# Dilated attention of a hybrid decoder step: turned rows first in each step, key rows copied by VectorE, first loads inside the projection, sample queries prepared in the last steps

## What is computed

```python
A_GROUPS = ((128, 1), (512, 4), (2048, 16))      # window, dilation; 8 heads of 64 each
def a_mixer(hn, pos, caches, w_in, q_g, k_g, w_out):
    n, T, _ = hn.shape
    qkv = (hn @ w_in).reshape(n, T, 3, N_GROUPS, A_HEADS, HEAD_DIM)
    for g, (window, dil) in enumerate(A_GROUPS):
        q = rope(rms_norm(qkv[:, :, 0, g], q_g[g]), pos)
        k = rope(rms_norm(qkv[:, :, 1, g], k_g[g]), pos)
        v = qkv[:, :, 2, g]
        if caches is None:
            o, lse = dilated_attention_prompt(q, k, v, window, dil)
            new = jnp.stack([k[:, T - keep:], v[:, T - keep:]], axis=1)
        else:
            o, lse, new = dilated_attention_sample(q, k, v, caches[g], window, dil)
...
    wts = jax.nn.softmax(jnp.stack(lses, axis=0), axis=0)
    o = jnp.einsum('gnthd,gnth->nthd', jnp.stack(outs, axis=0), wts.astype(outs[0].dtype))
    return o.reshape(n, T, A_HEADS * HEAD_DIM) @ w_out, rows
```

## Time and profile before

| what | us |
|---|---|
| median of 3 runs (lowest, highest) | 2953.03 (2950.44, 2971.38) |
| the profiled execution, its own time | 2953.42 |
| its span, first to last instruction | 2951.6 |
| busy in the span: TensorE, VectorE, ScalarE, GpSimd | 2710.9, 1736.7, 985.1, 725.0 |
| the stretch from the end of the projection to the first sample multiplication | 289.9 (520.4 to 810.26) |

### The profile page before, as it was taken

The page is one execution under the profiler, slowest core; times in us unless marked ns, Lnnn a source line. Parts: engine busy times, 40 slices in busy tenths (PEclk is TensorE's granted clock), DMA queues, the critical chain, the costliest instruction groups (busy, mean ns, idle before and its releaser), DMA issues.

```text
span 2951.6 us, 45737 instructions
## 1 busy us (share of the span) xinstructions
PE 2710.9 (92%) x17524; PEld 2636.7 (89%) x17524; DVE 1736.7 (59%) x2732; ACT 985.1 (33%) x1826; POOL 725.0 (25%) x342
## 2 busy tenths in 40 slices
PE   4999999788687999999999969698979999999997
PEld 3999999677676999999999958588979999999997
DVE  6887831555455555555555586695255655555655
ACT  3666631765303212221222245484222121112120
POOL 2111121333303222222222132173232222222220
PEclk7999999898788999999999989898999999999998
DMA  3322233443244343433354211344623444434441
GB/s 104 88 75 86 72 108 101 140 140 110 83 129 113 84 96 82 89 82 89 82 105 94 49 39 46 122 162 126 127 51 83 98 95 91 97 84 82 96 75 61
DMA packets 219856, 275.64 MB, mean 93 GB/s; under 512 B 29562, under 2 KB 191746, under 8 KB 217666
## 3 DMA queue, kind: packets, MB, share of 16 engines
q1 hardware_dynamic: 219746, 274.17, 37.2%
HBM read 237.90 MB, written 125.62 MB: 123 GB/s over the span
## 4 chain that ended last, share of the span: by engine, by line
PE 81%; DVE 8%; ACT 3%; DMA 3%; issue 2%; POOL 1%; SPq 1%; DVEq 0%; ACTq 0%; POOLq 0%
PE acc L347 23%; PE acc L349 23%; PE acc L348 23%; DVE arena L579 2%; PE aux L1869 2%; PE aux L1502 2%; PE acc L1461 1%; PE acc L1856 1%; PE acc L1470 1%; DVE arena L555 1%; PE acc L1839 1%; PE aux L635 1%; PE aux L634 1%; PE acc L2100 1%; POOL xl L533 1%
## 5 line engine op out<-in xcount | busy, mean ns | idle before, releaser
L347 PE MATMUL acc<-xh,w_hi 128*128 128x344 f32 x3504 | 1136.8, 324 | 63.4 <-DVE xl L533 36.3
L349 PE MATMUL acc<-xh,w_lo 128*128 128x344 f32 x3504 | 1127.8, 322 | 0.0
L348 PE MATMUL acc<-xl,w_hi 128*128 128x344 f32 x3504 | 1127.4, 322 | 0.0
L332 POOL TENSOR_TENSOR w_lo<-w_raw,w_hi 128x1024 fp32r<-128x1024 f32 x194 | 485.5, 2507 | 1799.9 <-ACT w_hi L322 1799.9
L347 PEld LDWEIGHTS acc<-xh,w_hi 128*128 128x128 f32 x3504 | 665.8, 190 | 82.0 <-issue 39.6
L349 PEld LDWEIGHTS acc<-xh,w_lo 128*128 128x128 f32 x3504 | 665.8, 190 | 0.0
L348 PEld LDWEIGHTS acc<-xl,w_hi 128*128 128x128 f32 x3504 | 665.8, 190 | 0.0
L849 DVE TENSOR_TENSOR hT<-hT,acc 128x1032 f32<-128x1032 f32 x184 | 226.3, 1230 | 387.6 <-PE acc L349 387.6
L322 ACT CAST w_hi<-w_raw 128x1024 fp32r<-128x1024 f32 x194 | 201.8, 1050 | 603.2 <-PE acc L349 504.3
L347 PE MATMUL acc<-f_hi,w_hi 128*128 128x344 f32 x1056 | 340.2, 322 | 11.1 <-DVE f_lo L1108 11.1
L349 PE MATMUL acc<-f_hi,w_lo 128*128 128x344 f32 x1056 | 339.5, 321 | 0.0
(11 more groups left out here) (254 smaller groups left out, 3184.6 us busy)
## 6 DMA issues: line engine op xcount, KB each, us to landing
out_a_w_sample<-in_cache_a_kv_w SPq DMA_DIRECT2D x23, 2848.0 KB
w_raw<-in_ffn_w_up SPq DMA_DIRECT2D x88, 512.0 KB, 3.8
scratch<-arena SPq DMA_DIRECT2D x46, 516.0 KB, 3.1
w_raw<-in_ffn_w_down SPq DMA_DIRECT2D x44, 512.0 KB, 3.5
w_raw<-in_a_w_in SPq DMA_DIRECT2D x36, 512.0 KB, 4.3
out_a_w_sample<-in_cache_a_kv_w SPq DMA_DIRECT2D x8, 2044.0 KB
arena<-in_cache_a_kv_w SPq DMA_DIRECT2D x24, 512.0 KB, 3.8
w_raw<-scratch SPq DMA_DIRECT2D x18, 512.0 KB, 3.7
```

Source lines behind the costliest of these rows:

```text
L332: pool.tensor_tensor(w_lo[:, slot, :], w_raw[:, slot, :], w_hi[:, slot, :].bitcast(F32), ALU.subtract).then_inc(lo_ready, 1)
L347: pe.matmul(out, whi, ahi, start=first, stop=False)
L348: pe.matmul(out, whi, alo, start=False, stop=False)
L349: return pe.matmul(out, wlo, ahi, start=False, stop=last)
```

## The change

It has four parts.

1. *Turned rows at the head of each step.* TensorE now turns value rows, key rows and statistics and spreads weights before the scores of unit k + 1, not behind them. VectorE makes half of unit k's masks, then the copies of value and key rows and the weighing, then the other half. The copy of key rows moves from ScalarE to VectorE (`key_rows_dve`). ScalarE's splits of keys and queries move from the head of the step to behind the second half of the exponentials.
2. *First loads in the projection.* Keys, queries and values of x = 0 are loaded at chunk 26 into the space of `rope` and `rinv`; ScalarE splits them at chunk 29 (`FIRST_SPLIT`), GpSimd two chunks later. x = 1 takes the place of x = 0 in the loads at chunk 35.
3. *The first scores' waits.* Units 0 and 1 wait only for those chunk thirds whose banks they take; VectorE clears the value tile between its half masks without waiting for the stores.
4. *Sample queries in the last steps.* `s_cols` is loaded at step 30 into `u_tail`; the queries are turned as jobs "sq" in steps 38 to 40 and split by VectorE; after step 42 (`A_TAIL` = 43) VectorE writes `s_sel` and TensorE makes the first two spreads; three of the first four cache loads are issued in steps 39 to 41, before the last statistics; the loads of the output weights no longer wait for the mixing.

```diff
         def proj_a_sp(sp):
-            with sp.Fori(0, A_CHUNKS // BODY - 1) as i:
+            with sp.Fori(0, 24 // BODY) as i:
...
-            for n in range(A_CHUNKS - BODY, A_CHUNKS):
+            for n in range(24, A_CHUNKS):
+                if n == 26:
+                    first_loads_sp(sp)
+                    first_values_sp(sp)
...
-                    sp.wait_ge(stored[0], 16 * 7)
-                    attn_a_loads(sp, 0, "q")
-                    attn_a_loads(sp, 0, "k")
+                    attn_a_loads(sp, 1, "q")
+                    attn_a_loads(sp, 1, "k")
...
+            if 38 <= k < 38 + NG:
+                names += [("sq", k - 38)]
...
-        ON_ACT = {"v": False, "k": True, "stat": True, "w": False}
+        ON_ACT = {"v": False, "k": False, "stat": True, "w": False, "sq": False}
...
         def raw_a(x, what):
-            return k_raw[x % 2] if what == "k" else q_raw
+
+            if x == 0:
+                return a_og["kqv".index(what)]
...
+        def first_loads_sp(sp):
+
+            sp.wait_ge(chunk_out, 3 * (CH + 24))
+            sp.wait_ge(stored[0], 16 * 12)
+            sp.wait_ge(stored[1], 16 * 12)
+            sp.dma_start(raw_a(0, "k"), rows_in_scratch(1, 0)).then_inc(DA.k_in[2], 16)
+            sp.dma_start(raw_a(0, "q"), rows_in_scratch(0, 0)).then_inc(DA.q_in[0], 16)
...
+                if k == 30:
+                    sp.dma_start(s_cols, scratch[0:A_CHUNKS, :, SEQ:T].rearrange("c p t -> p c t")).then_inc(ZA.cols, 16)
...
+                if k in (39, 40, 41):
+                    wait_job(sp, ("t", k - 2, 1))
+                    cache_rows_sp(sp, k - 39)
...
-                pe.wait_ge(acc_evac, 3 * CH_B)
+                pe.wait_ge(acc_evac, 3 * CH_B - (2 if u else 3))
...
-        def attn_a_pe(pe):
-            for k in range(-1, A_STEPS):
-                if 0 <= k + 1 < A_UNITS:
-                    scores_a_pe(pe, k + 1)
+        def attn_a_pe(pe, k0, k1):
+            for k in range(k0, k1):
...
+                if 38 <= k < 38 + NG:
+                    sample_rows_pe(pe, k - 38)
+                if 0 <= k + 1 < A_UNITS:
+                    scores_a_pe(pe, k + 1)
...
+        def key_rows_dve(v_, n):
+            cnt = K_JOBS[n % 4][3]
+            wait_job(v_, ("k", n))
+            if n < 2:
+                v_.wait_ge(lo_ready, U_AOUT + 2)
+            else:
+                v_.wait_ge(DA.k_out[n % 2], 16 * (n // 2))
+            v_.tensor_copy(k_stage[n % 2][:, 0:P * cnt], bank_a(("k", n))[:, 0:P * cnt]).then_inc(DA.out_dve, 1)
...
                 if k < A_UNITS:
-                    mask_a_dve(v_, k)
+                    mask_a_dve(v_, k, 0)
...
+                i, r = divmod(k, 10)
+                if 0 <= i < A_PAIRS and r in (2, 3, 6, 7):
+                    key_rows_dve(v_, 4 * i + (2, 3, 6, 7).index(r))
...
+                if 38 <= k < 38 + NG:
+                    sample_rows_dve(v_, k - 38)
+                if k < A_UNITS:
+                    mask_a_dve(v_, k, 1)
...
-                for x in starting(k + 3):
-                    if x:
-                        split_a_act(act, x, "k")
-                for x in starting(k + 2):
-                    if x:
-                        split_a_act(act, x, "q")
                 if 0 <= k < A_UNITS:
                     exps_a_act(act, k, 0)
-                i, r = divmod(k, 10)
-                if 0 <= i < A_PAIRS and r in (2, 3, 6, 7):
-                    key_rows_act(act, 4 * i + (2, 3, 6, 7).index(r))
...
+                for x in starting(k + 3):
+                    if x:
+                        split_a_act(act, x, "k")
+                for x in starting(k + 2):
+                    if x:
+                        split_a_act(act, x, "q")
```

More of the change, by code:

```diff
@@ L1578, in probs_a @@
             wait_job(eng, ("t", u, e))
+            if u == 0:
+                for n in range(2):
+                    eng.wait_ge(stored[n], 16 * A_CHUNKS // 2)
             if u >= 2:
@@ L2062, in sample_a_pe @@
                               start=True, stop=True)
-            pe.wait_ge(ZA.split, NG)
             for n in range(STEPS_A):
-                g, s2 = divmod(n, NS // 2)
                 if n >= 2:
-                    pe.wait_ge(ZA.multiplied, n - 1)
-                for e in range(2):
-                    for x in (s_qh, s_ql):
-                        mm = pe.matmul(acc[:, (2 * n + e) % 4, :], s_sel[:, 2 * s2 + e, :],
-                                       x[:, CROW * g:CROW * g + CROW], start=x is s_qh, stop=x is s_ql)
-                mm.then_inc(ZA.spread, 1)
+                    spread_pe(pe, n)
                 if 0 <= n - FIRST < PIECES // 2:
```

211 lines of the change are left out of this document (121 added, 90 removed).

## The result

The changed kernel takes **2982.24 us** (median of 8 runs, 2980.71 to 2984.28); the kernel before, on the same chip, 2954.51 us (median of 8). The ratio is 1.0075, 95% interval 1.0045 to 1.0105: 0.75% slower. Forecast were 2939.4 us and a range of 2919 to 2956; both are missed. The run with the profile took 2984.28 us, its span is 2982.5 us.

The account below looks back on a forecast made before the run. TensorE, with 81% of the chain and kept waiting in the attention, was taken to bound the kernel. Terms +1.7 + 1.2 - 2.5 - 2.0 + 0.7 - 1 - 11.7 = -13.6 us gave 2939.4 us from 2953.0; range 2919 to 2956.

Parts of the forecast that it names:

- start, to unit 10: From projection to unit 10's scores: earlier first scores, then waits for late query splits; +1.7 us (-6 to +5).
- block two: Attention units 10 to 19: old waits go, late splits add waits; 64.1 against 62.9 us, +1.2 us.
- block three: Attention units 20 to 29: old waits go, late splits add waits; 64.1 against 66.6 us, -2.5 us.
- units 30 to 38: Attention units 30 to 37, same trade of waits: 49.9 against 51.9 us, -2.0 us.
- last steps, statistics: Last attention steps: two cache loads now stand ahead of the last statistics' DMAs; +0.7 us (0 to +2).
- weights to first multiplication: Last weights, mixing and sample preparation: -1 us from a warmer clock, -11.7 us from sample work moved into the attention.
- the term for the clock: In each block of ten units: three waits lower TensorE's clock, 2.5 us added to 61.6 us.
- The wait that I let pay: At each group's scores: late splits cost 2 to 6 us, paid for by 9 us of old waits a block.
- The rival of late splits: Attention groups: late splits cost 2.5 us more each, 2967 us; sign turns at 1.2 us more a group; chance 0.12.
- The rival in which nothing takes the place of the waits: Attention blocks: splits run in ScalarE's idle time, so 26.2 us of waits simply go; 2912 us, chance 0.13.
- The sample term: Between mixing's end and first sample multiplication: preparation already done in the attention, only a product and hand-over left; -11.7 us.
- The third rival: Twelve sample steps: late cache rows or output weights stretch them, 8 us given back, 2947 us; chance 0.15.

Follow-up runs that it names:

- e5: Kernel after with two VectorE writes of 1024 columns ahead of the copy that leads to the last stage's first product: 2956.28 us.
- e6: Kernel before with three VectorE writes of 1024 columns ahead of the copy that leads to the last stage's first product: 2989.44 us.
- e1: Kernel after with ScalarE's splits of the next group's keys and queries ahead of the step's first exponentials again: 2919.81 us, ratio to before 0.9883.
- e12: e1 plus two dense pieces behind the last stage's first sparse products, and ScalarE's next output-weight split held until after the sample's small product: 2915.08 us.

## Why the prediction was wrong

By its own steps, forecast against measured in the profiled executions:

| step | forecast | measured |
|---|---|---|
| start, to unit 10 | +1.7 | +3.0 |
| block two | +1.2 | +5.9 |
| block three | -2.5 | +1.6 |
| units 30 to 38 | -2.0 | +1.1 |
| last steps, statistics | +0.7 | +3.6 |
| weights to first multiplication | -12.7 | -9.8 |
| the twelve sample steps, to the last stage | 0 | -2.1 |
| the last stage | not priced | +27.3 |

**The step that failed most** is one that the prediction doesn't have: it ends its sum at the sample steps and takes all behind them to keep its length, so the last stage is a term put at nothing without a reason. That stage starts 3.25 us later and took 82.3 instead of 55.0 us, since the clock stayed at its lower level; that a shift of its start alone does this is shown by e5 and e6. The earlier trace rows end at 849.50, ahead of it, and the prediction cites no row of the stage. In the profiled executions the kernel after lies 44.2 us behind the forecast at line 549 (30.6 + 13.6), and 27.3 of them are this; in the medians it is 42.8 us (2982.2 - 2939.4).

**The blocks.** The mechanism was right: waits for low halves at eleven groups, 25 to 50 us in all forecast, 40.9 measured; 3.9, 6 and 2 us for the three groups of a block forecast, 4.24, 5.27 and 1.02 measured. Mis-sized was above all the term for the clock, in a block that was forecast at 64.1 us and took 68.8. TensorE's busy time multiplied by the mean granted clock is nearly the same in all versions with rows first, 54.51 x 0.84 = 45.8 us in the kernel after, 50.77 x 0.91 = 46.2 in e1; so a block of the kernel after would take about 45.8 + 14.3 idle = 60.1 us at the full clock (61.6 forecast), and the clock costs about 8.7 us, where I had added 2.5. That is an estimate, since the mean also counts idle time. Not all of it belongs to the late splits: reckoned in the same way e1 loses 4.6 us a block (50.77 - 46.2) beside 5.5 us idle. I had taken the 2.5 us from the one block of before whose clock was 0.92; the one beside it was 0.85.

**The wait that I let pay.** The forecast set the late splits against the waits that go and came to -3.3 us for three stretches. The runs price them apart: 42.6 us for the late splits, against 31.1 us that all the rest gains. The 2 to 6 us a group were the forecast's own prices, and they were right for the waits (40.9 us over eleven groups is 3.7). The rival of late splits, which I gave 0.12, named the right place but asked for 2.5 us more a group. Up to unit 38 the kernel after is 13.1 us behind the forecast (+11.5 against -1.6), or 1.2 us a group: half of that rival, and just where its sign turns. The rival in which nothing takes the place of the waits (2912 us) is e1 and e12: 2919.8 and 2915.1 us, and it needed only the splits where they were.

**Smaller steps.** First scores at 519.63, within 1 us of the last projection product, right. The chain of the start was read well too: unit 4 at 537.7 and unit 8 at 558.2 forecast, 535.9 and 558.4 measured. The wait of the statistics for the exponentials (3.5 us in the earlier trace rows) was to go and is 4.2 us, at line 1507; those of the weights for the value rows (4.9 us) were to shrink to 1 us each and are 5.7 us in three, at line 1514, in e1 too. The last steps cost 2.9 us more than forecast; e1 has 34.6 us there (721.45 to its first weights at 756.08) against 30.52 before, so the late splits are not the cause. Two sample turnings wait 1.1 us each for VectorE (line 1576), and the two cache loads stand ahead of the statistics; which of these costs how much was not tried. The weights' stage ran at 0.50 as before, the forecast gain of 1 us did not come. The sample term lacked the 2.1 us of the slow product: GpSimd's low half of the output weights, 7.3 us behind the mixing before, follows it at once now and fell on the product; that this comes from the earlier loads was not run. The third rival did not come: from the first multiplication to the last stage the kernel after takes 45.06 us, the one before 47.15. But that stretch was 49.8 us in e1, with the same loads and by the clock, so the 2.1 us gained there are luck.

## What to carry to other kernels

An edit that removes waits and one that adds them can lie in the same step of an engine's program; test them apart, since here the net 11.5 us lost at unit 38 hide 31 us gained and 43 us lost by six moved lines. Read every stage behind the change as well: where dense and sparse products take turns, a shift of the start by 1 to 3 us can decide between two speeds, and two dense pieces back to back took the chance out here for 3 to 5 us. A wait of TensorE costs more than its length: from e1 to the kernel after the waits for low halves grow by 36.2 us (4.7 to 40.9), and unit 38 comes 42.6 us later.

## What the chip showed that I had not expected

TensorE can be busy without a gap for over 70 us and keep the lower of its two clock levels (kernel after, 860.66 to 934.5), when half of the time in each turn goes to products of two columns, and it can lose the higher level in the midst of such products (kernel before, 895.6). Delaying the last stage by 2.5 us with writes of VectorE made the kernel before 34 us slower, delaying it by 1.3 us made the kernel after 26 us faster; in the stage alone that is 27 us either way, by nothing that the runs show but the moment at which the same products start. And a product of 96 columns that takes 0.26 us alone takes 2.38 us beside a GpSimd instruction of 2.34 us.
